# Memory brought in transposed as well, and its row factor moved from the memory to the keys and values made from it

## The reference, cut to what matters

```python
def rmsnorm(x, g):
    y = xf * lax.rsqrt(jnp.mean(xf * xf, axis=-1, keepdims=True) + NORM_EPS)
    return (y * g.astype(jnp.float32)).astype(x.dtype)

def memory_xattn(h, mem, mem_norm_g, w_xq, w_xkv, w_xo):
    m = rmsnorm(mem, mem_norm_g)
    q = jnp.einsum('bsd,dn->bsn', h, w_xq).reshape(B, S, XATTN_HEADS, XATTN_HEAD_DIM)
    kv = jnp.einsum('bmd,dn->bmn', m, w_xkv).reshape(B, M, 2, XATTN_HEADS, XATTN_HEAD_DIM)
    ...
```

## Time and profile before

| what | value |
|---|---|
| median of 3 runs | 1427.05 us (1427.02 to 1427.57) |
| the profiled execution, its own time | 1423.45 us |
| its span, first to last instruction | 1421.7 us |
| mean granted TensorE clock | 0.997 |
| DVE busy | 57% of the span |
| ACT busy | 46% |
| POOL busy | 59% |
| DMA, mean | 116 GB/s |

### The profile page before, as it was taken

One profiled execution on the slowest core, in us unless ns is written; L12 is line 12 of the kernel. 1 busy time (PEld: TensorE's weight loads), 2 busy tenths in 40 slices (PEclk: granted clock), 3 DMA queues, 4 the chain that ended last, 5 costly groups with the idle time before them and its releaser, 6 DMA issues. The chain is left out here.

```text
span 1421.7 us, 18322 instructions
## 1 busy us (share of the span) xinstructions
PE 1381.4 (97%) x6696; PEld 1159.3 (82%) x6696; DVE 810.4 (57%) x999; ACT 656.9 (46%) x1207; POOL 834.7 (59%) x631
## 2 busy tenths in 40 slices
PE   8999999999999999999999899999999999999998
PEld 6977779888889787888887688888888888878776
DVE  3576643134445574431645876666656664488966
ACT  5567635445335664553544533333323323444355
POOL 4648857741446677595246665555545554477884
PEclk9999999999999999999999999999999999999999
DMA  8401044513323101463144043332333325973234
GB/s 277 166 23 38 23 149 134 166 49 127 99 66 93 38 16 52 149 186 120 50 126 172 30 141 111 112 106 88 110 112 112 111 82 199 311 237 115 79 103 156
DMA packets 99145, 164.66 MB, mean 116 GB/s; under 512 B 8560, under 2 KB 40688, under 8 KB 99056
## 3 DMA queue, kind: packets, MB, share of 16 engines
q1 hardware_dynamic: 99056, 163.48, 35.1%
HBM read 134.88 MB, written 28.57 MB: 115 GB/s over the span
## 5 line engine op out<-in xcount | busy, mean ns | idle before, releaser
L749 POOL TENSOR_TENSOR w_lo<-w_raw,w_hi 128x512 fp32r<-128x512 f32 (+2 forms) x236 | 307.0, 1314 | 228.7 <-ACT w_hi L904 227.8
L1909 PE MATMUL ps<-h_hi_P,w_hi 128*128 128x512 f32 x616 | 241.2, 392 | 5.8 <-DVE h_lo_P L1350 3.1
L1910 PE MATMUL ps<-h_lo_P,w_hi 128*128 128x512 f32 x616 | 240.4, 390 | 0.0
L1911 PE MATMUL ps<-h_hi_P,w_lo 128*128 128x512 f32 x616 | 240.3, 390 | 0.0
L904 ACT ACTIVATE w_hi<-w_raw 128x512 fp32r<-128x512 f32 (+2 forms) x236 | 140.9, 608 | 197.0 <-PE ps L1911 180.8
L749 POOL TENSOR_TENSOR w_lo<-w_sum,w_hi 128x512 fp32r<-128x512 f32 x88 | 118.4, 1349 | 115.9 <-ACT w_hi L904 115.9
L749 POOL TENSOR_TENSOR w_lo<-a_raw,w_hi 128x512 fp32r<-128x512 f32 x77 | 111.9, 1455 | 74.2 <-ACT w_hi L904 74.1
L1909 PEld LDWEIGHTS ps<-h_hi_P,w_hi 128*128 128x128 f32 x616 | 116.0, 188 | 32.5 <-issue 4.7
L1909 PE MATMUL ps<-w_hi,act_hi 128*128 128x512 f32 (+2 forms) x384 | 140.6, 366 | 1.5 <-POOL w_lo L749 1.5
L1911 PE MATMUL ps<-w_hi,act_lo 128*128 128x512 f32 (+2 forms) x384 | 139.8, 364 | 0.0
L1910 PE MATMUL ps<-w_lo,act_hi 128*128 128x512 f32 (+2 forms) x384 | 139.8, 364 | 0.0
(11 more groups left out here) (242 smaller groups left out, 3046.1 us busy)
## 6 DMA issues: line engine op xcount, KB each, us to landing
gu_raw<-in_w_gate_up SPq DMA_DIRECT2D x22, 1024.0 KB, 5.5
a_raw<-a_mem SPq DMA_DIRECT2D x77, 256.0 KB, 2.7
w_raw<-in_w_xkv SPq DMA_DIRECT2D x64, 256.0 KB, 3.2
a_mem<-down_sum SPq DMA_DIRECT2D x44, 256.0 KB, 2.6
wd<-in_w_down SPq DMA_DIRECT2D x44, 256.0 KB, 5.6
a_mem<-act_t SPq DMA_DIRECT2D x33, 256.0 KB, 2.1
w_raw<-in_w_out SPq DMA_DIRECT2D x32, 256.0 KB, 2.6
w_raw<-in_w_xq SPq DMA_DIRECT2D x32, 256.0 KB, 2.9
```

The source lines that it names most:

```text
L749: return nc.gpsimd.tensor_tensor(out, whole, hi.bitcast(F32), ALU.subtract)
L1909: nc.tensor.matmul(out, s_hi, m_hi, start=start, stop=False, skip_group_check=more)
L1910: nc.tensor.matmul(out, s_hi, m_lo, start=False, stop=False, skip_group_check=more)
L1911: return nc.tensor.matmul(out, s_lo, m_hi, start=False, stop=stop, skip_group_check=more)
```

## The change

The memory is brought in twice: as it is (m_tok, only for its row sums of squares) and transposed (mt_raw, 1 MB in 4 transfers of 256 KB whose rows are 1 KB). The gain is a number per partition now and comes with another small load, so m_gain and its broadcast go. ACT makes the hi parts (8 activations of 128x256 with the gain as scale), DVE the lo parts (8 scalar_tensor_tensor of 128x256). The memory's 16 transposes, two norms, four hi and four lo parts from PSUM are gone. The row factors are kept in columns 4 and 5 of rstd. They are applied to the values as a scale per partition at their evacuation, and to the keys by a product with m_row, which two 128x128 products on TensorE and one copy on DVE make. For the keys each tile takes three steps now: a multiply from PSUM into kx_f (DVE), the hi part from kx_f (ACT), the lo part from kx_f (DVE), which frees the bank.

The order of the lists changes with it: on DVE the eight lo parts stand ahead of `add_to_x(g, "out0", 0)`, and on ACT the eight hi parts stand between the last four out0 calls of `weights_hi`.

```diff
-                sp.dma_start(m_gain[:], mem_norm_g.partition_broadcast(P)).then_inc(mem_in, 16)
+                for r in range(4):
+                    sp.dma_start(mt_raw[:, 2 * r:2 * r + 2, :],
+                                 mem_t[g, 2 * r * P:(2 * r + 2) * P, :].rearrange("(k p) m -> p k m", p=P)
+                                 ).then_inc(mt_in, 16)
@@ ACT
-                act.wait_ge(mem_in, (g + 1) * (MT + 1) * 16)
+                act.wait_ge(mem_in, (g + 1) * MT * 16)
                 for t in range(MT):
-                    square(g, None, m_tok[:, t, :], junk2[:, t, :], t, D)
-                root(g, 2 * T + MT, 0, MT)
-                weights_hi(g, "out0", 4, KD)
-                weights_hi(g, "out1", 0, 2)
-                for t in range(MT):
-                    transposed_hi(g, "mem", t, mt_hi)
-                weights_hi(g, "out1", 2, KD)
+                    square(g, None, m_tok[:, t, :], junk2[:, t, :], T + t, D)
+                root(g, 2 * T + MT, T, MT)
+                for k in range(KD):
+                    if k % 2 == 0:
+                        weights_hi(g, "out0", 4 + k // 2, 5 + k // 2)
+                    act.wait_ge(mt_in, 4 * 16 * (g + 1))
+                    nc.scalar.activation(mt_hi[:, k, :], mt_raw[:, k, :], ACT.Copy,
+                                         scale=mem_gain[:, k:k + 1]).then_inc(mt_hi_done.sem, 1)
+                weights_hi(g, "out1")
...
@@ DVE
+                invert(g, 2, MT, T)
+                for k in range(KD):
+                    dve.wait_ge(mt_hi_done.sem, mt_hi_done.at(g, k + 1))
+                    nc.vector.scalar_tensor_tensor(out=mt_lo[:, k, :], in0=mt_raw[:, k, :], scalar=mem_gain[:, k:k + 1],
+                                                   in1=mt_hi[:, k, :].bitcast(F32), op0=ALU.mult,
+                                                   op1=ALU.subtract).then_inc(mt_ready.sem, 1)
                 add_to_x(g, "out0", 0)
-                dve.wait_ge(mem_in, (g + 1) * (MT + 1) * 16)
-                invert(g, 2, MT)
-                for t in range(MT):
-                    normed(m_tok[:, t, :], m_tok[:, t, :], t, m_gain[:]).then_inc(h_ready.sem, 1)
...
+                dve.wait_ge(psum_full.sem, psum_full.at(g, TEN["mem"] + 2 * MT))
+                nc.vector.tensor_copy(m_row[:], bank(TEN["mem"], M)).then_inc(psum_free.sem, 2 * MT)
                 add_to_x(g, "out1", 1)
...
+                        nc.vector.tensor_tensor(kx_f[:, f, :], bank(ten, M), m_row[:],
+                                                ALU.mult).then_inc(kx_scaled.sem, 1)
+                    for f in range(4 if i < 2 else 0):
+                        lo_out(g, HI[name] + f, TEN[name] + f, kx_lo[:, 4 * i + f, :], kx_f[:, f, :],
+                               kx_hi[:, 4 * i + f, :])
...
@@ TensorE
-                def memory():
+                def memory_row():
+                    pe.wait_ge(rstds.sem, rstds.at(g, 3))
+                    claim(g, TEN["mem"] + 2 * MT - 1)
                     for t in range(MT):
-                        transpose_tokens(g, TEN["mem"] + 2 * t, t + 1, m_tok[:, t, :])
-                by_tokens(g, "out1", act_hi, act_lo, T, OUT_ROWS, before={2: memory})
-                pe.wait_ge(psum_free.sem, psum_free.at(g, TEN["mem"] + 2 * MT))
+                        last = nc.tensor.matmul(ps[:, TEN["mem"] % BANKS, t * P:(t + 1) * P],
+                                                rstd[:, T + t:T + t + 1].broadcast_to([P, P]), ident[:],
+                                                start=True, stop=True)
+                    last.then_inc(psum_full.sem, 2 * MT)
+                by_tokens(g, "out1", act_hi, act_lo, T, OUT_ROWS, before={2: memory_row})
+                pe.wait_ge(mt_ready.sem, mt_ready.at(g, KD))
```

More of the change, by code:

```diff
@@ L96, in key_value_columns, with build @@
     return np.ascontiguousarray(keys), np.ascontiguousarray(w[:, :, nope_dim:].reshape(rows, -1))
-def build(nc, x, x_t, mem, tables, ln_pair, ln_cols, w_in, q_norm_g, w_q, kv_norm_g, w_k, w_v, w_fnet, w_out, ln_x_g,
-          mem_norm_g, w_xq, w_xkv, w_xo, w_gate_up, w_down, final_norm_g, y):
+def build(nc, x, x_t, mem, mem_t, tables, ln_pair, ln_cols, w_in, q_norm_g, w_q, kv_norm_g, w_k, w_v, w_fnet, w_out, ln_x_g,
+          w_xq, w_xkv, w_xo, w_gate_up, w_down, final_norm_g, y):
     G, S, D = x.shape
@@ L265, in build @@
         qx_lo = at("qx_lo", R + 48, [P, KD, S], F32R)
-        m_gain = at("m_gain", R + 32, [P, D])
+        kx_f = at("kx_f", R + 32, [P, 4, M])
         x_gain = at("x_gain", R + 36, [P, D])
@@ L270, in build @@
         m_tok = at("m_tok", R + 64, [P, MT, D])
+        mt_raw = at("mt_raw", R + 56, [P, KD, M])
+        m_row = at("m_row", R + 88, [P, M])
         mt_hi = at("mt_hi", R + 72, [P, KD, M], F32R)
@@ L307, in build @@
         mix_gain = stats[:, 96:96 + KD]
+        mem_gain = stats[:, 96 + KD:96 + 2 * KD]
         rowmax = stats[:, 32:40]
@@ L339, in build @@
         rstds = Count(sem("rstds"), 5, 1)
-        h_ready = Count(sem("h_ready"), T + MT)
+        h_ready = Count(sem("h_ready"), T)
+        mt_in = sem("mt_in")
+        mt_hi_done = Count(sem("mt_hi_done"), KD)
+        mt_ready = Count(sem("mt_ready"), KD)
+        kx_scaled = Count(sem("kx_scaled"), KD)
         cols_in = sem("cols_in")
@@ L447, in build @@
         for name, count in (("chan01", 2), ("chan23", 2), ("positions", FG), ("c", CQ + CK),
-                            ("vv", T), ("mem", 2 * MT), ("xk0", 4), ("n2t0", 2), ("xk1", 4), ("n2t1", 2), ("xv0", MT),
+                            ("vv", T), ("xk0", 4), ("n2t0", 2), ("xk1", 4), ("n2t1", 2), ("xv0", MT),
                             ("n2t2", 2), ("n2t3", 2), ("xv1", MT), ("xq0", 4), ("xq1", 4)):
@@ L573, in load_first_tile @@
                 sp.dma_start(w_raw[:, w % RING, 0:src.shape[1]], src).then_inc(raw_full[w % RING].sem, 16)
-            sp.dma_start(stats[:, 96:96 + KD], ln_cols[:, :]).then_inc(cols_in, 16)
+            sp.dma_start(stats[:, 96:96 + 2 * KD], ln_cols[:, :]).then_inc(cols_in, 16)
             for k in range(KD):
@@ L1113, in _ @@
                         if i < 2:
-                            hi_out(g, ten, kx_hi[:, 4 * i + f, :], bank(ten, M))
-                        else:
-                            hi_out(g, ten, vx_hi[:, f, (i - 2) * BANK:(i - 1) * BANK], bank(ten))
+                            act.wait_ge(kx_scaled.sem, kx_scaled.at(g, 4 * i + f + 1))
+                            copy(kx_hi[:, 4 * i + f, :], kx_f[:, f, :]).then_inc(hi_done.sem, 1)
+                        else:
+                            act.wait_ge(psum_full.sem, psum_full.at(g, ten + 1))
+                            nc.scalar.activation(vx_hi[:, f, (i - 2) * BANK:(i - 1) * BANK], bank(ten), ACT.Copy,
+                                                 scale=rstd[:, T + f:T + f + 1]).then_inc(hi_done.sem, 1)
                     weights_hi(g, name, KD - 1, KD)
@@ L1576, in _ @@
                 pair_scale(g, PAIRS - 1)
-                add_to_x(g, "out0", 0)
-                dve.wait_ge(mem_in, (g + 1) * (MT + 1) * 16)
-                invert(g, 2, MT)
-                for t in range(MT):
-                    normed(m_tok[:, t, :], m_tok[:, t, :], t, m_gain[:]).then_inc(h_ready.sem, 1)
[L1583 to L1587, removed]
+                invert(g, 2, MT, T)
[4 more added lines that the diff above has]
+                                                   op1=ALU.subtract).then_inc(mt_ready.sem, 1)
+                add_to_x(g, "out0", 0)
+                dve.wait_ge(psum_full.sem, psum_full.at(g, TEN["mem"] + 2 * MT))
+                nc.vector.tensor_copy(m_row[:], bank(TEN["mem"], M)).then_inc(psum_free.sem, 2 * MT)
                 add_to_x(g, "out1", 1)
@@ L1596, in _ @@
                                TEN[f"n2t{i - 1}"] + 2 if i >= 1 else None)
-                    for f in range(4 if i < 2 else MT):
+                    if i < 2:
+                        dve.wait_ge(psum_free.sem, psum_free.at(g, TEN[name] if i == 0 else TEN["xk0"] + 4))
+                    for f in range(4 if i < 2 else 0):
                         ten = TEN[name] + f
[L1599 to L1603, removed]
+                        dve.wait_ge(psum_full.sem, psum_full.at(g, ten + 1))
+                        nc.vector.tensor_tensor(kx_f[:, f, :], bank(ten, M), m_row[:],
+                                                ALU.mult).then_inc(kx_scaled.sem, 1)
+                    for f in range(4 if i < 2 else 0):
+                        lo_out(g, HI[name] + f, TEN[name] + f, kx_lo[:, 4 * i + f, :], kx_f[:, f, :],
+                               kx_hi[:, 4 * i + f, :])
+                    for f in range(0 if i < 2 else MT):
+                        ten = TEN[name] + f
+                        o = (slice(None), f, slice((i - 2) * BANK, (i - 1) * BANK))
+                        dve.wait_ge(hi_done.sem, hi_done.at(g, HI[name] + f + 1))
+                        nc.vector.scalar_tensor_tensor(out=vx_lo[o], in0=bank(ten), scalar=rstd[:, T + f:T + f + 1],
```

(11 more changed lines are left out.)

## The result

| | before | after |
|---|---|---|
| median, runs side by side | 1427.03 us | 1446.81 us |
| ratio, 95% interval | | 1.0143 (1.0132 to 1.0155) |
| the profiled execution, its own time | 1423.45 us | 1446.86 us |
| its span | 1421.7 us | 1445.1 us |
| mean granted TensorE clock | 0.997 | 0.989 |

The change makes the kernel 19.8 us slower. The forecast was 1452 us, 5 us too much, and 1446.8 lies in its range.

A forecast was written before the change was run, and what follows sets the result against it. TensorE, busy 97% of the span, was taken as the bound. Pause 22.2, slow clock 5.1 and keys 2.6, less 5.25 gained, add 24.65 us to 1427.05: 1451.7, rounded to 1452, range 1441 to 1458.

The forecast's parts named there:

- What bounds the kernel, and where the change meets it: Whole kernel: TensorE, busy 97% of the span, bounds it; other engines' work counts only where TensorE waits.
- the rival without the slow clock: Behind the pause before out1, TensorE's clock stays at 2.4 GHz: 1446.6 us; chance 0.15.
- Part 1, the gain: At the memory ahead of the keys, two 128x128 products replace the transposes on TensorE: 5.25 us gained.
- Part 2, the pause: Between out0 and out1, TensorE waits for DVE's adds behind the lo parts: 11.1 us a group, 22.2 in all.
- The rival without turns: DVE's lo parts slip between POOL's instructions, ACT sets the pace: pause 8.5 us, xk0's seam free, 1443.9 us; chance 0.14.
- Part 3, the clock: At out1's start, matmuls run at 1.2 GHz's pitch after the pause: 2.56 us a group, 5.1 in all.
- Part 4, the keys: xk1's fourth tile waits for xk0's second bank: 1.3 us a group, 2.6 in all; values cost nothing.
- The sign that I had named for it: At xk1's start, TensorE would wait 1 to 2 us.
- The sum: Whole kernel: 22.2 + 5.1 + 2.6 - 5.25 = 24.65 us slower, from median 1427.05 to 1451.7 us.
- POOL as the bound of the keys: At the keys, lo parts take POOL's time and TensorE waits: 3 to 6 us more, about 1456; chance 0.1.
- Faster: At out1, the adds come in time, so only the gain at the memory is left: 1421.8 us; chance 0.03.

The follow-up runs named there:

- the kernel with the filler: Changed kernel plus 40 matmuls of 512 columns, results unused, ahead of out1 in TensorE's list: 1443.55 us, ratio 1.0117.
- the two kernels on POOL: Changed kernel with ACT's four weight tiles behind the eight hi parts: 1439.09 us; changed kernel with out0 adds behind four of eight lo parts: 1443.25 us.

## Why the prediction was right, by its own steps

- **What bounds the kernel, and where the change meets it.** Right. TensorE's list was full, and each term stood at the place that was named. The measured 1446.8 us is also what the rival without the slow clock had named (1446.6); by the number alone one could take that rival for the cause, and only the pitch of 0.43 us behind the pauses and the kernel with the filler rule it out.
- **Part 1, the gain.** 5.25 us forecast. With the pause taken away, the stretches a are 55.56 us against 60.86: 5.30.
- **Part 2, the pause.** 11.1 us a group forecast, 10.70 and 10.79 measured. The steps of the chain, in their order: from the issue of m_tok to the first square 4.97 us (4.9 forecast), root and squares 3.71 (3.71), ACT's eight hi parts and four weights 5.36 (5.5), the last lo part 2.68 behind the last hi part (3.1), the first add and TensorE's start 0.87 (0.8). The order's part of it is shown by moving the adds in both kernels, the turns' part by the two kernels on POOL. The rival without turns (0.14) falls with them. The Trainium skill (SBUF — State Buffer, "SBUF: two separate sides") says that of a VectorE instruction with two SBUF inputs and a GpSimd one that reads SBUF, whichever starts first holds the ports that the two share for its whole instruction; by that rule the pause would have been 0.8 us longer a group. The trace differs, with shorter turns: a lo part that met a w_lo ended 0.3 us behind it, not 0.47, and four w_lo took 5.49 us, 0.45 us more than alone, about 0.15 us for each of the three lo parts between them. In the kernel with the adds first, where both engines work on without a pause, seven w_lo took 9.89 us, 1.41 each instead of 1.26.
- **Part 3, the clock.** The mechanism was right, and the rival in which the clock stays (0.15) fell. The size was off: 5.1 us forecast, 3.3 measured (19.50 more in a, less 21.49 of pauses, plus 5.30 of gain). I took all 12 slow matmuls of the start; here eight and seven were slow. This is the largest miss of the sum. It is not only a matter of the kernel, as the pauses of the experiments show (group 0, group 1; lost is what the 16 intervals behind the pause took beyond 16 x 0.227 us):

  | kernel | pause, us | slow matmuls | lost, us |
  |---|---|---|---|
  | after | 10.70, 10.79 | 8, 7 | 1.8, 1.5 |
  | before, adds behind the norms | 7.90, 7.69 | 14, 8 | 2.9, 1.8 |
  | weight tiles behind the hi parts | 7.15, 6.56 | 13, 9 | 2.9, 2.0 |
  | adds after four lo parts | 9.12, 9.30 | 10, 11 | 2.2, 2.5 |
  | after, TensorE kept busy | 1.73, 1.84 | 0, 0 | 0.1, 0.1 |

  A pause cost 1.5 to 2.9 us, and the two longest cost less than most; what sets the number is not shown. My 2.56 for one pause lies within this, and the changed kernel's profiled execution has the two cheapest. The Trainium skill (TensorE: Matmul & The Clock Gate, "What's actually happening") calls 1.2 GHz the idle engine's state, and the trace agrees, with a granted clock of 0.53 behind a pause of 10.70 us. One reading was wrong: the rival was supported by "TensorE's short waits cost no slow matmuls", but the trace of the kernel before itself has eight slow ones behind a wait of 1.86 us (last section).
- **Part 4, the keys.** The place and the cause were right, the size was not: 2.6 us forecast, 1.64 measured. I let the first lo part wait half a w_lo and each next a whole one with 0.3 us between; in the trace the second is done 0.6 us earlier than that. The sign that I had named for it, 1 to 2 us of waiting at xk1's start, did not come: it was 0.73 us. The values cost nothing, as forecast: b is before's to 0.02 us once the keys' bank is freed early.
- **The sum.** 24.65 us forecast, 21.14 in the stages of the profiled executions, 19.8 between the medians. The stages miss the forecast by 3.5 us: 0.7 in the pauses, 1.8 in the clock, 1.0 in the keys, all in the same direction, so no errors cancelled. The 1.3 us between the stages and the medians are within what varies from execution to execution: the rest of the span is 1197.4 to 1199.8 us among the profiled ones.
- **The other rivals.** POOL as the bound of the keys (0.1) did not happen; leaving out the keys' step showed no time that POOL had cost. Faster (0.03) was the fate of the kernel with the adds in front: 1421.8 was named for it, 1421.9 measured. That agreement is luck: 1421.8 leaves out the 1.6 us of the keys' seam, and before ran 1.2 us lower beside it. Against before it is 3.95 us faster, where the rival had 5.25 and my expectation of that run, with the seam, 3.75.

## What to carry to other kernels

In an in-order list, an instruction that frees a buffer for the bounding engine belongs ahead of every preparation that isn't due yet: here the same four adds decided between 4 us faster and 20 us slower. Where a value is copied out of a scarce buffer, free the buffer at the copy and not at the last use of the value. And when VectorE and GpSimd both read two operands from SBUF, count a small VectorE instruction at the length of the GpSimd one that it can meet: here a lo part at a pitch of 0.40 us alone came at 1.41 us beside w_lo of 1.26 us.

## What the runs showed of the hardware

TensorE's clock can fall after shorter idle times than the pause here. In the changed kernel's profiled execution, in a part of group 0 that the change doesn't touch, TensorE idles 1.64 us, runs transposes for 2.4 us and idles 1.91 us; then matmuls come at 0.43 us for 3.4 us, with a granted clock of 0.51. The first view is TensorE's timeline, the second that by stretches:

```profile
80.03 2.40 PE L2186 MATMUL ps<-ident,z 128*128 128x128 f32 x20 [1.64 <-DVE z L1384]
84.78 0.47 PE L1933 MATMUL ps<-c_hi,w_hi 128*128 128x512 f32 x1 [1.91 <-DVE c_lo L1365]
...
85.56 0.63 PE L1933 MATMUL ps<-c_hi,w_hi 128*128 128x512 f32 x1
85.99 0.63 PE L1934 MATMUL ps<-c_lo,w_hi 128*128 128x512 f32 x1
...
85.50:89.00 3.50, 3.50 (x10) 2.70 (x10) 2.09 (x4) 0.00 (x0) 0.00 (x0) 0.51 0.00 0
```

The same place of the kernel before, with idle times of 0.56 and 1.90 us, ran at full pitch in its profiled execution. From it I had read that short waits cost no slow matmuls, and overlooked another place of the same trace, 809.62, where eight are slow:

```profile
809.62 0.62 PE L1909 MATMUL ps<-h_hi_P,w_hi 128*128 128x512 f32 x1 [1.86 <-issue]
810.04 0.63 PE L1910 MATMUL ps<-h_lo_P,w_hi 128*128 128x512 f32 x1
...
809.50:813.00 3.50, 3.38 (x8) 2.65 (x9) 2.51 (x5) 2.03 (x3) 1.36 (x1) 0.54 0.84 290
```

The length of a short wait doesn't decide it. In six of the ten traces the wait ahead of group 0's transposes is 1.63 or 1.64 us: three have a fall of the clock there (the changed kernel, the repeat of the kernel with the adds first, and the one with the adds after four lo parts), and three have none. In the other four it is 0.55 or 0.56 us: the kernel with unscaled keys has eight slow matmuls, and three kernels have none. The kernel with the adds first, run twice, had 0.56 us and full pitch once, 1.64 us and a granted clock of 0.50 during the transposes the other time. Every one of the ten traces has at least one such stretch outside the two stages, and eight slow matmuls take 1.6 us more than at full pitch; so these stretches and that wait make a part of the spread from execution to execution. What brings them on is not shown.
